# Delta rule on quarters of the array: independent 64x64x64 products issued as diagonal and off-diagonal pairs

## The reference, cut to what matters

```python
lower = where(strict, (k*beta) @ k.T * decay, 0)
tmat = inverse(I + lower)
u, w = tmat @ (v * beta), tmat @ (k * beta * exp(gcum))
qk = where(causal, q @ k.T * decay, 0)
# along the chunks
v_new = u - w @ S
o = (q * exp(g)) @ S + qk @ v_new
S = S * exp(g_last) + (k * exp(g_last - g)).T @ v_new
```

## Time and profile before

| | |
|---|---|
| runs | 1440.89, 1436.83, 1439.99 us; median 1439.99 |
| profiled execution, its own time | 1439.63 us |
| its span in the trace | 1438.0 us |
| granted clock, mean of the core | 0.989 |
| PE busy, share of the span | 96% |
| the phase `delta_rule` | 351.0 to 482.2 us of the span |

### The profile page before, as it was taken

The page is one execution under the profiler, slowest core; times in us unless marked ns, Lnnn a source line. Parts: engine busy times, 40 slices in busy tenths (PEclk is TensorE's granted clock), DMA queues, the critical chain, the costliest instruction groups (busy, mean ns, idle before and its releaser), DMA issues.

```text
span 1438.0 us, 32177 instructions
## 1 busy us (share of the span) xinstructions
PE 1375.4 (96%) x13125; PEld 1281.9 (89%) x13125; DVE 924.2 (64%) x1494; ACT 519.5 (36%) x906; POOL 474.3 (33%) x431
## 2 busy tenths in 40 slices
PE   6999999998999899889988999999999999999996
PEld 6899999988899666548878999999999999999996
DVE  6429999832888556665677555555455556677786
ACT  5422222242333335444544323322232332443552
POOL 4145000011987132300044555666454543000014
PEclk9999999999999999999999999999999999999999
DMA  7222121131543446262212333333233335656533
GB/s 222 63 61 49 46 56 46 37 94 42 156 138 105 121 141 174 68 195 88 88 45 59 111 101 92 111 112 99 81 94 89 111 106 185 203 178 184 163 87 143
DMA packets 145433, 156.14 MB, mean 109 GB/s; under 512 B 18956, under 2 KB 113415, under 8 KB 145272
## 3 DMA queue, kind: packets, MB, share of 16 engines
q1 hardware_dynamic: 118050, 140.83, 32.2%
q10 hardware_dynamic: 24006, 12.12, 3.2%
q0 software_dynamic: 3232, 1.14, 0.7%
HBM read 121.02 MB, written 33.35 MB: 107 GB/s over the span
## 4 chain that ended last, share of the span: by engine, by line
PE 51%; DVE 2%; DMA 1%; ACT 1%; SPq 0%; issue 0%; POOL 0%; DVEq 0%; ACTq 0%
PE mf_ps L3404 29%; PE mf_ps L3431 13%; PE mf_ps L3328 7%; PE mf_ps L3444 2%; PE mf_ps L3460 0%; DMA mo_o_raw<-in_w_out_dram 0%; PE mf_ps L3396 0%; PE mf_ps L3340 0%; DMA hidden_operands<-ff_t_sum 0%; DVE ff_w_lo L3041 0%; DMA ff_m_raw<-hidden_operands 0%; ACT h_t_hi L2890 0%; DVE ff_p_lo L3095 0%; DVE h_t_lo L3046 0%; DVE h_lo L3046 0%
## 5 line engine op out<-in xcount | busy, mean ns | idle before, releaser
L3041 DVE TENSOR_TENSOR ff_w_lo<-ff_sum,ff_w_hi 128x512 fp32r<-128x512 f32 x87 | 87.3, 1004 | 85.9 <-ACT ff_w_hi L2867 84.0
L3404 PE MATMUL mf_ps<-h_lo,ff_w_hi 128*128 128x258 f32 x680 | 137.0, 283 | 0.0
L3404 PE MATMUL mf_ps<-h_t_hi,ff_w_hi 128*128 128x258 f32 x672 | 136.4, 284 | 0.0
L3404 PE MATMUL mf_ps<-h_t_hi,ff_w_lo 128*128 128x258 f32 x672 | 135.2, 283 | 0.0
L902 PE MATMUL pc_main<-h_hi,in_whi 128*128 128x344 f32 x528 | 116.5, 329 | 1.7 <-PEq L88 1.7
L902 PE MATMUL pc_main<-h_hi,in_wlo 128*128 128x344 f32 x528 | 112.4, 321 | 0.0
L902 PE MATMUL pc_main<-h_lo,in_whi 128*128 128x344 f32 x528 | 112.2, 321 | 0.0
L3431 PE MATMUL mf_ps<-ff_m_hi,ff_s_hi 128*128 128x258 f32 x528 | 107.0, 284 | 0.6 <-DVE ff_m_lo L3101 0.6
L3431 PE MATMUL mf_ps<-ff_m_hi,ff_s_lo 128*128 128x258 f32 x528 | 106.8, 284 | 0.0
L3431 PE MATMUL mf_ps<-ff_m_lo,ff_s_hi 128*128 128x258 f32 x528 | 106.4, 283 | 0.0
L3404 PEld LDWEIGHTS mf_ps<-h_lo,ff_w_hi 128*128 128x128 f32 x680 | 105.8, 189 | 0.0
(11 more groups left out here) (565 smaller groups left out, 3500.9 us busy)
## 6 DMA issues: line engine op xcount, KB each, us to landing
ff_m_raw<-hidden_operands SPq DMA_DIRECT2D x66, 258.0 KB, 2.7
fs_keys<-in_cache_k_dram SPq DMA_DIRECT2D x64, 192.0 KB, 2.8
at_values<-in_cache_v_dram SPq DMA_DIRECT2D x64, 192.0 KB, 2.6
hidden_operands<-ff_t_sum SPq DMA_DIRECT2D x44, 258.0 KB, 3.7
ff_raw<-in_w_gate_dram SPq DMA_DIRECT2D x22, 512.0 KB, 6.4
ff_raw<-in_w_up_dram SPq DMA_DIRECT2D x22, 512.0 KB, 5.2
ff_a<-in_w_down_dram SPq DMA_DIRECT2D x44, 256.0 KB, 3.2
in_raw<-in_w_in_dram ACTq DMA_DIRECT2D x20, 512.0 KB, 3.9
```

Of the source, the lines that this page charges most:

```text
L3041: dve.tensor_tensor(w_lo[q % 4][:], stationary(*tasks[q]), w_hi[q % 4][:].bitcast(F32), ALU.subtract).then_inc(w_lo_cut, 1)
L3404: last = pe.matmul(into[:, g], a[q % 4][:, k], b[:, k, g * TQ:(g + 1) * TQ], start=(fresh and k == 0 and i == 0), stop=(k == KH - 1 and i ...
```

## The change

The four quarters of the array are used in place of the two diagonal ones. Two groups of 12 products that don't depend on each other are issued interleaved: two products on the diagonal, then two off the diagonal, whose result lies on the other half of the partitions. The groups paired are levels 1 with 4 and 2 with 5, level 3 with the turned keys of the block ahead, u with w, w times state with q times state, and the state's update with the values' part of the output. In each pair the two groups write different banks of PSUM. What lands on the other half is brought back by the copy that existed already, in two instructions of 64 partitions each: `copy_x` of levels 3, 4 and 5, `copy_w` and `copy_out`. A joint group waits for the inputs of both before its first product. The values are turned before the keys, and `rows_done` counts twice per block. `from_state` waits for all its inputs first. The diff, without its unchanged lines:

```diff
...
+CROSSED = (3, 4, 5)
...
         def copy_x(c, lv):
-            act.mul(x[s][:], heads(2 * s), -1.0).then_inc(x_copied[s], 1)
+            if lv not in CROSSED:
+                act.mul(x[s][:], heads(2 * s), -1.0).then_inc(x_copied[s], 1)
+                return
+            for e in range(2):
+                last = act.mul(x[s][half(e)], heads(2 * s)[half(1 - e)], -1.0)
+            last.then_inc(x_copied[s], 1)
         def copy_query(c):
...
-            act.mul(neg_w[:], heads(stage[1]), -1.0).then_inc(w_copied, 1)
+            for e in range(2):
+                last = act.mul(neg_w[half(e)], heads(stage[1])[half(1 - e)], -1.0)
+            last.then_inc(w_copied, 1)
         def copy_out(c):
-            act.copy(m.yT[:, 2:2 + PAIRS, c * P:(c + 1) * P].rearrange("p i (b t) -> p i b t", b=2),
-                     ps[:, out, 0:W].rearrange("p (b i t) -> p i b t", b=2, i=PAIRS)).then_inc(o_copied, 1)
+            for e in range(2):
+                last = act.copy(m.yT[half(e), 2:2 + PAIRS, c * P:(c + 1) * P].rearrange("p i (b t) -> p i b t", b=2),
+                                ps[half(1 - e), out, 0:W].rearrange("p (b i t) -> p i b t", b=2, i=PAIRS))
+            last.then_inc(o_copied, 1)
...
         def scale_keys(c):
-            dve.wait_ge(rows_done, c + 1)
+            dve.wait_ge(rows_done, 2 * c + 2)
         def scale_values(c):
-            dve.wait_ge(rows_done, c + 1)
+            dve.wait_ge(rows_done, 2 * c + 1)
         def decay_keys(c):
-            dve.wait_ge(rows_done, c + 1)
+            dve.wait_ge(rows_done, 2 * c + 2)
...
     def _(pe):
-        def lower_times_t(c, lv):
-            s = c % 2
+        def wait_lower(c, lv):
-                pe.wait_ge(t_turned[s], of_turn(c, 0))
+                pe.wait_ge(t_turned[c % 2], of_turn(c, 0))
-                pe.wait_ge(t_added[s], of_level(c, lv - 1))
-            for n, e in pair_up:
-                last = pe.matmul(heads(2 * s)[half(e), n], lt[c % 3][half(e), n], tt[c % 3][half(e), 0, n], start=True,
-                                 stop=True)
-            last.then_inc(x_done[s], 1)
+                pe.wait_ge(t_added[c % 2], of_level(c, lv - 1))
+
+        def lower_of_heads(c, lv, n):
+            for e in range(2):
+                to = half(1 - e if lv in CROSSED else e)
+                last = pe.matmul(heads(2 * (c % 2))[to, n], lt[c % 3][half(e), n], tt[c % 3][half(e), 0, n],
+                                 start=True, stop=True)
+            if n == 2 * PAIRS - 1:
+                last.then_inc(x_done[c % 2], 1)
+
+        def lower_times_t(*of):
+            for c, lv in of:
+                wait_lower(c, lv)
+            for n in range(2 * PAIRS):
+                for c, lv in of:
+                    lower_of_heads(c, lv, n)
         def next_t(c, lv):
...
-        def turn_rows(c):
+        def turn_rows(c, beside):
-            for bank, t in zip(stage, (T_KB, T_VB)):
-                for n, e in pair_up:
-                    last = pe.matmul(heads(bank)[half(e), n], m.proj[half(e), t + n % PAIRS, tokens(c, n)],
-                                     m.ident[half(e), half(e)], start=True, stop=True)
-            last.then_inc(rows_done, 1)
+            for n in range(2 * PAIRS):
+                turn_of_heads(c, stage[1], T_VB, n)
+            if beside is not None:
+                wait_lower(beside, 3)
+            for n in range(2 * PAIRS):
+                turn_of_heads(c, stage[0], T_KB, n)
+                if beside is not None:
+                    lower_of_heads(beside, 3, n)
+
+        def turn_of_heads(c, bank, t, n):
+            for e in range(2):
+                last = pe.matmul(heads(bank)[half(e), n], m.proj[half(e), t + n % PAIRS, tokens(c, n)],
+                                 m.ident[half(e), half(e)], start=True, stop=True)
+            if n == 2 * PAIRS - 1:
+                last.then_inc(rows_done, 1)
         def values_and_keys(c):
-            for n, e in pair_up:
-                pe.matmul(heads(stage[0])[half(e), n], tt[c % 3][half(e), 1, n], vb[half(e), n], start=True, stop=True)
-            for n, e in pair_up:
-                last = pe.matmul(heads(stage[1])[half(e), n], ke[half(e), n], tt[c % 3][half(e), 1, n], start=True,
-                                 stop=True)
+            for n in range(2 * PAIRS):
+                for e in range(2):
+                    pe.matmul(heads(stage[0])[half(e), n], tt[c % 3][half(e), 1, n], vb[half(e), n], start=True,
+                              stop=True)
+                for e in range(2):
+                    last = pe.matmul(heads(stage[1])[half(1 - e), n], ke[half(e), n], tt[c % 3][half(e), 1, n],
+                                     start=True, stop=True)
         def from_state(c, b):
...
-            for i in range(PAIRS):
-                for e in range(2):
-                    last = pe.matmul(ps[half(e), update, i * HD:(i + 1) * HD], neg_w[half(e), b * PAIRS + i],
-                                     m.state[half(e), i], start=True, stop=True)
-            last.then_inc(ws_done, 1)
-                    pe.matmul(heads(out)[half(e), b * PAIRS + i], m.state[half(e), i],
+                    last = pe.matmul(ps[half(e), update, i * HD:(i + 1) * HD], neg_w[half(e), b * PAIRS + i],
+                                     m.state[half(e), i], start=True, stop=True)
+                if i == PAIRS - 1:
+                    last.then_inc(ws_done, 1)
+                for e in range(2):
+                    pe.matmul(heads(out)[half(1 - e), b * PAIRS + i], m.state[half(e), i],
...
-            last.then_inc(s_done, 1)
-            for i in range(PAIRS):
+                if i == PAIRS - 1:
+                    last.then_inc(s_done, 1)
-                    last = pe.matmul(heads(out)[half(e), b * PAIRS + i], v_new[half(e), i],
+                    last = pe.matmul(heads(out)[half(1 - e), b * PAIRS + i], v_new[half(e), i],
+            if lo is not None and lo > 0:
+                spread_query(lo)
+            lower_times_t(*[(c, lv) for c, lv in ((lo, 1), (hi, 4)) if c is not None])
-                lower_times_t(lo, 1)
-            elif lo is not None:
-                spread_query(lo)
-                lower_times_t(lo, 1)
-            if hi is not None:
-                lower_times_t(hi, 4)
...
-            if lo is not None:
-                lower_times_t(lo, 2)
-            if hi is not None:
-                lower_times_t(hi, 5)
+            lower_times_t(*[(c, lv) for c, lv in ((lo, 2), (hi, 5)) if c is not None])
-                turn_rows(hi)
-            if lo is not None:
-                lower_times_t(lo, 3)
+                turn_rows(hi, lo)
+            elif lo is not None:
+                lower_times_t((lo, 3))
```

## The result

| | before | changed |
|---|---|---|
| median, 11 runs each | 1439.61 us | 1446.40 us |
| lowest and highest | 1436.83, 1445.04 | 1443.45, 1449.16 |
| ratio, with its 95% interval | | 1.0051 (1.0039 to 1.0062) |
| the profiled execution, its span | 1439.63, 1438.0 us | 1447.92, 1446.2 us |
| granted clock, mean of the core | 0.989 | 0.979 |

The change costs 6.8 us. The page of the changed kernel answers to the earlier trace rows: TensorE's share fell from 96% to 94% with the same 13125 matmuls.

A forecast was written before the change was run, and what follows sets the result against it. PE's own rate was taken to bound the rounds (14.3 us each). Rounds 1 to 6 at -10.4, round 8's earlier start -0.5 and tail +0.4 gave -10.5 against 1439.63: 1429.1 us, 8-in-10 range 1425.5 to 1437.

The forecast's parts named there:

- PE's round is then ... 10.1 us, and PE stops being the bound.: Full rounds: 288 paired instructions at 14.6 ns instead of 29.2 bring PE's round from 14.3 to 10.1 us.
- The forecast's -10.4 for rounds 1 to 6: Six intervals between takes of level 3: 87.3 us before, 76.9 after, with middle rounds of 13.1 us.
- the third rival: Full rounds: quarters overlap, but late keys or breaks in PE's instruction supply eat half; rounds 14.0, 1433.5 us, chance 0.15.
- The walk through the round: One full round followed step by step: new waits of about 0.4 us beside VectorE's 12.66, so 13.1 us a round.
- Rounds 0 and 1 keep their length: Start of the stage: no change in these two rounds, because GpSimd ran there without a break.
- The tail, "+0.4": Rounds 8 and 9: bound by latency, half copies +1.6, values first -0.5, paired u and w -0.7, together +0.4 us.
- The half copies were counted as +1.6: Tail: half copies of x4, x5, neg_w and the last output add 0.4 us each, +1.6 in all.
- The credits for values first and paired u and w (-1.2): Tail: turning the values before the keys gains 0.5 us, pairing u with w gains 0.7.
- I charge nothing for PE's new idle time: Granted clock: stays at 1.00 in rounds from 362 us on even with PE partly idle, so 0 us cost.
- no overlap: Rival for paired products: quarters of the same rows don't overlap, 29.2 ns stays, +1.0 us a round; 1446.7 us, chance 0.12.
- 25 ns floor: Rival for paired products: each start takes at least 25 ns, rounds of 14.1 us; 1434.5 us, chance 0.08.
- GpSimd's 12.8 us as a bound: Full rounds: GpSimd needs 12.80 us from one first_t to the next, so no round goes below 12.8.

The follow-up runs named there:

- after_onecopy: The changed kernel with each crossed copy done by one ScalarE instruction over all 128 partitions, output not the reference's: 1441.36 us, ratio 1.0019 to the kernel before.
- onecopy_held: The changed kernel with whole crossed copies (output not the reference's) and 15 unused wide products in the last two rounds and at the stage's end: 1437.90 us, ratio 0.9999.
- after_fewer: The changed kernel without 10 of 12 products in turned keys, turned values and gram, output not the reference's: 1435.80 us, ratio 0.9983 to the kernel before.
- before_waits: The kernel before with 480 already satisfied waits added to PE in next_t: 1445.34 us, ratio 1.0049 to the kernel before.
- before_nokeys: The kernel before without the loads of the cached keys of samples 1 to 7: 1435.87 us, ratio 0.9976 to the kernel before.
- after_waits: The changed kernel with 480 already satisfied waits added to PE in next_t, four runs only: 1455.79 us, ratio 1.0127 to the kernel before.
- after_held: The changed kernel with 15 unused wide products where PE waits in the last two rounds and at the stage's end: 1437.83 us, ratio 1.0005 to the kernel before.

## Why the prediction was wrong, point by point

- **The step that failed**: "PE's round is then ... 10.1 us, and PE stops being the bound." The price per instruction was right; the sum left out that PE must also be handed its 924 instructions a round, and that takes 15.1 us beside the keys. Pairing leaves the count unchanged, so it can't shorten this. The forecast's -10.4 for rounds 1 to 6 became -0.4. The supply did stand in the third rival, with the sign of it read as a disturbance that would eat half; the trace of before held the size already (four starved blocks, at 4.37 us on the mean), and 14.53 us of array time was about as long. Shown by after_onecopy and onecopy_held, where the copies' waits go and the gaps at the block ends take their place, and in keeping with after_fewer.
- **The walk through the round** gave waits of 0.4 us. Its copies were priced at 0.39 us behind one another; half copies take 0.49 each, a pair 0.98. In the full rounds this is covered by the supply (after_onecopy). In the tail and in round 0 it isn't.
- **"Rounds 0 and 1 keep their length"**: round 0 is 1.8 us longer, of which PE's waits for x are 0.5 (1.7 against 1.2). The rest goes with a lower granted clock (0.71 against 0.83 on the mean of the stretch) and does not belong to the change: before_waits and before_nokeys, with whole copies and no pairs, show 10.50 us at 0.73 and 10.30 at 0.74 there, and after_fewer and after_waits, with half copies and pairs, 9.72 and 9.84 at 0.84. Round 1 is 1.1 shorter (13.54 against 14.66).
- **The tail, "+0.4"**: measured +4.1 behind the start of round 7. The half copies were counted as +1.6, but the pair costs 0.5, not 0.4, each time; PE waits 1.9 and 0.8 us for "issue" at L1774 and L1789, in the last u and w and state steps, and it runs at 1.2 GHz from 478.8 to 492.4 us. The credits for values first and paired u and w (-1.2) are not to be seen.
- **"I charge nothing for PE's new idle time"**: in the rounds the clock stayed at 1.00, as said (in after_waits, with more idle time, one round ran at 0.90). Behind the tail it did not, and the attention took 3.4 us more. That filling the tail gives 6.6 us back is shown by after_held, and that it can hold the clock and shorten the attention by the traces of after_onecopy and onecopy_held; how the 6.6 us are shared between the clock and the rest is not.
- **The rivals**: the two with a price for the quarters (no overlap, 25 ns floor) are refuted by 14.8 ns. That the first had nearly the measured time (1446.7 us) is luck: the quarters did overlap, and the loss came from elsewhere. The third had the right mechanism at half its size.
- **Kept**: VectorE at 12.1 to 13.0 us in rounds 2 to 6, ScalarE 2.6 us a round busier (4.93 to 7.49), and GpSimd's 12.8 us as a bound of about the right size, though after_fewer does not part it from the supply of its 800 instructions.

Open: why the packet of the next block starts only 1.6 us into a block (fewer instructions were tried only by leaving out work, not by a version that computes the same with fewer), and the part of after_held's gain that the clock doesn't explain.

## What to carry to other kernels

Count TensorE's instructions, matmuls and weight loads, beside its busy time: here 256 of them took 3.8 to 4.2 us on the mean of the starved blocks, 15 to 16.4 ns each, so this stage of small products, with an array time near that, gained nothing from running them side by side. Gaps "issue" every 256 instructions, with a packet of the instruction queue in each, are the sign, and a few of them in the profile before mark how near the limit is. What should help is fewer, larger instructions, which no run here tried without leaving work out. And where a change leaves a tail of short waits, look at the granted clock of the stage behind it.

## What the runs showed of the hardware that was not expected

- PE's instructions arrived in packets of 16 KB, one per 256, in starved blocks with 2.5 us (no key transfers) or 2.7 to 3.1 us (with them) from a block's first instruction to the end of the packet, and 1.3 to 1.5 more until PE went on. Beside the keys' transfers the packet of a starved block took 1.16 us, without them 0.98.
- Four quarters of the array ran 64x64x64 float32 products at 14.8 ns per instruction (48 matmuls and their weight loads in 0.71 us).
- A ScalarE copy of 64 partitions by 384 took 0.49 us, as much as one of 128 partitions.
- Wide products that nobody uses, put into waits of the last rounds, cost no time in any of the four kernels that had them (all at 0.9984 to 1.0005 of the kernel before).
